# Three projections of a two-block layer with tokens on the partitions, and top-k moved to follow its scores

## The reference, cut

```python
# first block, after two attentions on h = rms(x) @ w_in
mix = concat([rms(o_sb, g1), rms(o_mla, g2)]) @ w_o          # output projection, 1024 x 1024
x = x + rms(mix, g_post_mix)
u = causal_conv3(rms(x, g_pre_ffn) @ w_up)                   # 1024 x 5632
gate, val = split(u)
x = x + rms((gelu(gate) * val) @ w_down, g_post_ffn)         # 2816 x 1024
g = sigmoid(rms(x, g_ple_gate) @ w_ple_gate + b_ple_gate)    # 1024 x 1024
x = x + rms(g * (p @ w_ple), g_post_ple)                     # 256 x 1024
# second block
mod = silu(c) @ mod_w + mod_b                                # 1024 x 6144: six rows of scales and shifts
h = rms(x, norm1_g) * (1 + sc1) + sh1
# z = h @ w_in_2 feeds a 31-tap convolution, a pool mixer, and an attention that keeps, of each
# token's index scores, the 64 best keys
x = x + g1 * (concat(parts) @ w_out_2)
# 32 experts of width 512, two for each token
x = x + g2 * moe(rms(x, norm2_g) * (1 + sc2) + sh2)
return rms(x, final_g)
```

## Time and profile before

| | |
|---|---|
| time, median of 3 runs | 1084.17 us (1083.63 to 1092.6) |
| time of the profiled execution | 1083.46 us |
| its span, first to last instruction | 1081.4 us |
| TensorE busy | 847.7 us (78%) |
| VectorE, ScalarE, POOL busy | 322.7, 284.2, 141.1 us |
| mean granted TensorE clock | 0.913 of full speed |
| DMA | 297.44 MB, mean 275 GB/s |

### The profile page before, as it was taken

How to read it: one execution, slowest core, us unless ns; L and a number is a source line. 1 busy time by engine, 2 the same in 40 slices (tenths; PEclk the granted TensorE clock), 3 DMA queues, 4 the chain that set the end, 5 groups by cost and what they waited for, 6 DMA issues and landing times.

```text
span 1081.4 us, 12688 instructions
## 1 busy us (share of the span) xinstructions
PE 847.7 (78%) x5392; PEld 577.1 (53%) x5392; DVE 322.7 (30%) x674; ACT 284.2 (26%) x541; POOL 141.1 (13%) x152
## 2 busy tenths in 40 slices
PE   7998688799998998959977979866657665766564
PEld 6855366699998995838765945312113131212111
DVE  2215422567666424054754131000001010000001
ACT  2325321366566442223534121000000000000011
...
GB/s 364 376 145 100 167 212 223 166 161 205 182 160 123 210 22 428 178 78 79 137 174 1 396 188 360 429 428 427 428 427 428 428 427 427 429 427 429 427 427 179
DMA packets 22671, 297.44 MB, mean 275 GB/s; under 512 B 2640, under 2 KB 2896, under 8 KB 4560
## 3 DMA queue, kind: packets, MB, share of 16 engines
...
HBM read 295.50 MB, written 1.05 MB: 274 GB/s over the span
## 4 chain that ended last, share of the span: by engine, by line
PE 57%; DMA 28%; DVE 8%; ACT 4%; issue 1%; POOL 1%; SPq 0%; DVEq 0%; POOLq 0%
PE ps L186 56%; DMA ring<-in_exps 28%; DVE yT L214 1%; ACT ar L200 1%; DVE ar L206 1%; DVE hT L214 1%; ACT yT L200 1%; DVE rb L275 1%; ACT ar L197 1%; DVE ar L1086 0%; ACT sq L200 0%; DMA ring<-in_win 0%; DVE yT L206 0%; DVE misc L1083 0%; DVE misc L615 0%
## 5 line engine op out<-in xcount | busy, mean ns | idle before, releaser
L186 PE MATMUL ps<-ring,sq 128*32 128x512 f32 x976 | 140.8, 712 | 90.3 <-DMA ring<-in_exps 88.6
L186 PE MATMUL ps<-hT,ring 128*128 128x256 f32 (+2 forms) x672 | 152.2, 388 | 12.9 <-DMA ring<-in_win 6.8
L186 PE MATMUL ps<-ring,ar 128*32 128x512 f32 (+1 forms) x696 | 100.9, 691 | 58.8 <-DMA ring<-in_exps 35.2
L186 PEld LDWEIGHTS ps<-hT,ring 128*128 128x128 f32 (+2 forms) x672 | 128.6, 192 | 34.2 <-issue 7.6
L186 PEld LDWEIGHTS ps<-ring,sq 128*32 128x32 f32 x976 | 29.8, 120 | 197.1 <-DMA ring<-in_exps 138.0
L186 PE MATMUL ps<-fr 128*128 128x256 f32 x792 | 103.2, 287 | 7.0 <-DVE fr L206 7.0
L186 PE MATMUL ps<-fr,fr_h 128*128 128x256 f32 x792 | 101.8, 284 | 4.0 <-POOL fr_h L217 2.1
L186 PEld LDWEIGHTS ps<-fr 128*128 128x128 f32 x792 | 99.7, 196 | 7.4 <-issue 6.4
L186 PEld LDWEIGHTS ps<-fr,fr_h 128*128 128x128 f32 x792 | 98.5, 192 | 4.5 <-POOL fr_h L217 2.3
L200 ACT ACTIVATE ar<-ps 128x768 f32<-128x768 f32 (+1 forms) x21 | 15.1, 717 | 281.1 <-PE ps L186 276.0
L206 DVE TENSOR_TENSOR ar<-ar,ps 128x512 f32<-128x512 f32 (+1 forms) x10 | 6.4, 641 | 267.8 <-PE ps L186 267.8
...
## 6 DMA issues: line engine op xcount, KB each, us to landing
...
```

The source lines that it names most:

```text
L186: return pe(lambda e: e.matmul(o, l, r, start=start, stop=stop, skip_group_check=True), *waits, inc=inc)
```

## The change

The output projection, down and gate now load the activations (128 features x 128 tokens) and stream 512 columns of the weights, so the result has tokens on the partitions, in four banks (token half j, column half n): `wo_part`, `down` and the gate's loops. The norm's sum then runs along a row: `token_square` squares with an accumulator, `token_diagonal` adds two numbers per token, takes root and reciprocal of one column, and writes the identity scaled by the factors. `to_features` multiplies the copied result (`mt`, in `yT`) by that diagonal, which turns it back and scales it, and `add_turned` adds it to `xT` with the gain, on VectorE. The next norm's sums take the loaded squares against one column of ones (`x_sums`), root and reciprocal are of two columns (`row_root`), and `over_rows` spreads the factors over the partitions. The gate's factor and bias are applied on its result, the bias from a new input `brow`.

Slot 5 moves to the last place of `mla_fill`, 6, 7 and 8 to 11 between the new steps; `mod_sum(7)` goes behind up's first slot and `mod_sum(11)` behind the first projection of the second block. Four weight parts of up are made ahead instead of two. The six slots of down are asked for at once, and the loads of `pT` and `brow` behind them wait for the end of up. `modulated` adds its shift on ScalarE, and the first projection of the second block goes over features first. The top-k's rounds are placed on VectorE behind the index scores: four there, three behind the latent norms' sums, one behind the latents. At the end a table load for the root is issued before the last squares; an activation that loaded it in the last expert group goes. The functions `Norm` and `residual` are removed.

```diff
         def mla_fill(i):
             if i == 1:
                 sb_group()
-            elif i < 6:
+            else:
                 mod_slot(i - (i > 1))
...
+        def row_root(b, dim, c, t):
+            m = misc[:, c:c + 4]
+            read[b] = t = a_fn(m[:, 0:2], ps[:, b, 0:2], ACT.Sqrt, t, t_eps, bias=eps, scale=1.0 / dim)
+            return m[:, 2:4], dve(lambda e: e.reciprocal(m[:, 2:4], m[:, 0:2]), t)
+        def over_rows(b, r, *waits):
+            for j in range(2):
+                t = mm(bank(b, 128 * j, 128 * j + 128), r[:, j:j + 1].broadcast_to([128, 128]), ident, True, True, *waits, inc=j)
+            return t
+        part, fac, mt, dg = misc[:, 56:60], misc[:, 72:78], yT, rb[:, 0, :]
+        def token_square(j, n, src, *waits):
+            i = 2 * j + n
+            return a_fn(sq[:, 512 * i:512 * i + 512], src, ACT.Square, *waits, accum_out=part[:, i:i + 1])
+        def token_diagonal(j, *waits, beside=None):
+            t = v_tt(fac[:, j:j + 1], part[:, 2 * j:2 * j + 1], part[:, 2 * j + 1:2 * j + 2], ALU.add, *waits)
+            if beside:
+                beside()
+            t = a_fn(fac[:, 2 + j:3 + j], fac[:, j:j + 1], ACT.Sqrt, t, t_eps, bias=eps, scale=1.0 / 1024)
+            t = dve(lambda e: e.reciprocal(fac[:, 4 + j:5 + j], fac[:, 2 + j:3 + j]), t)
+            return v_ts(dg[:, 128 * j:128 * j + 128], ident, fac[:, 4 + j:5 + j], None, ALU.mult, None, t, d_con)
+        def leave(j, n, b, t, t_sq, t_mt, t_dg, *waits):
+            i = 2 * j + n
+            t_sq[j, n] = token_square(j, n, bank(b), t)
+            def copy():
+                read[b] = t_mt[j, n] = v_copy(mt[:, 512 * i:512 * i + 512], bank(b), t_sq[j, n], *waits)
+            if n:
+                t_dg[j] = token_diagonal(j, t_sq[j, 0], t_sq[j, 1], beside=copy)
+            else:
+                copy()
+        def to_features(j, TB, *waits):
+            out = []
+            for k in range(8):
+                b = TB[k // 2]
+                o = (k % 2) * S + 128 * j
+                t = mm(bank(b, o, o + 128), mt[:, 1024 * j + 128 * k:1024 * j + 128 * k + 128], dg[:, 128 * j:128 * j + 128], True, True,
+                       read[b] if j == 0 else None, *waits, inc=k % 2)
+                out += [t] if k % 2 else []
+            return out
+        def add_turned(TB, gain, tt):
+            out = []
+            for k in range(8):
+                b, x = TB[k // 2], tile(xT, k)
+                t = v_stt(x, bank(b, (k % 2) * S, (k % 2) * S + S), gain(k), x, ALU.mult, ALU.add, tt[0][k // 2], tt[1][k // 2], d_cols)
+                read[b] = t
+                out.append(t)
+            return out
+        def x_square(i, tx_):
+            return a_fn(sq[:, i * 512:(i + 1) * 512], xT[:, i * 512:(i + 1) * 512], ACT.Square, tx_[2 * i + 1])
+        def x_sums(i, b, tok):
+            for k in (2 * i, 2 * i + 1):
+                for j in range(2):
+                    o = k * S + 128 * j
+                    t = mm(ps[:, b, j:j + 1], sq[:, o:o + 128], ones[:, 0:1], k == 0 and j == 0, k == 7, tok,
+                           read[b] if k == 0 and j == 0 else None, inc=int(k % 2 == 1 and j == 1))
+            return t
...
+        def wo_part(j, n, ks):
+            for k in ks:
+                o = k * S + 128 * j
+                t = mm(bank(2 * j + n), hT[:, o:o + 128], w_o[n].ap(k * 512, 512), k == 0, k == 7, w_o[n].ready, tg[k],
+                       read[2 * j + n], inc=int(k == ks[-1]))
             return t
+        for n in range(2):
+            for j in range(2):
+                wo_part(j, n, range(4))
...
+        t_sq, t_mt, t_dg = {}, {}, {}
+        for n in range(2):
+            for j in range(2):
+                t = wo_part(j, n, range(4, 8))
+                leave(j, n, 2 * j + n, t, t_sq, t_mt, t_dg)
+            w_o[n].free(t)
+        t_oT.append(t)
+        ahead += [weight_parts(w_up.ap(512 * k, 512), p_tt, w_up.ready) for k in range(2, 4)]
+        TB = (6, 7, 0, 1)
+        tt = [to_features(j, TB, t_dg[j], t_mt[j, 0], t_mt[j, 1]) for j in range(2)]
+        t_x = add_turned(TB, lambda k: col("g_post_mix", k), tt)
+        sqd = [x_square(i, t_x) for i in range(4)]
+        mod_slot(6)
+        for i in range(4):
+            t = x_sums(i, 2, sqd[i])
+        r, t_r = row_root(2, 1024, 116, t)
+        t = over_rows(3, r, t_r, read[3])
+        tx = []
         for k in range(8):
+            th = v_stt(tile(yT, k), tile(xT, k), col("g_pre_ffn", k), bank(3, 0, S), ALU.mult, ALU.mult, t, tt)
+            tx.append(split(tile(yT, k), tile(fr, k, XH), tile(fr, k, XL), v_tt, th))
+        read[3] = th
+        mod_slot(7)
...
+                                  weight_parts(w.ap(512 * k, 512), p_tt if k % 4 == 3 or (j == 0 and k % 2) else v_tt, w.ready))
...
+            if j == 0:
+                mod_sum(7)
...
+        t_up = t
+        DB = {(0, 0): 2, (0, 1): 3, (1, 0): 6, (1, 1): 7}
+        w_d = [stream("wdown", i, (4 if i < 5 else 2) * 1024) for i in range(6)]
+        pT, eT, brow = 0, 512, 2560
+        d_p = sp.dma(lambda e: e.dma_start(ar[:, pT:pT + 512], A["pT"]), sem("s_p"), 16, t_up)
+        d_b = sp.dma(lambda e: e.dma_start(ar[:, brow:brow + 1024], A["brow"]), sem("s_b"), 16, t_up)
...
+        def down(f, j, n, wh, wl, t_w):
+            fh, fl = (fr[:, o + S * f + 128 * j:o + S * f + 128 * j + 128] for o in (FH, FL))
+            o = bank(DB[j, n])
+            mm(o, fh, wh, f == 0, False, t_w, t_f[f], read[DB[j, n]])
+            mm(o, fh, wl, False, False)
+            return mm(o, fl, wh, False, f == 21, inc=1)
+        t_sq, t_mt, t_dg = {}, {}, {}
+        for f in range(20):
+            for n in range(2):
+                i, wh, wl, t_w = down_parts(f, n)
+                for j in range(2):
+                    t = down(f, j, n, wh, wl, t_w)
+                wp_free[i] = t
+                next(behind, None)
+            if f % 4 == 3:
+                w_d[f // 4].free(t)
+            if f == 8:
+                a_fn(misc[:, 2:3], eps, ACT.Sqrt, t_eps)
+        for n in range(2):
+            wps = [down_parts(f, n) for f in (20, 21)]
+            for j in range(2):
+                for f, (i, wh, wl, t_w) in zip((20, 21), wps):
+                    wp_free[i] = t = down(f, j, n, wh, wl, t_w)
+                leave(j, n, DB[j, n], t, t_sq, t_mt, t_dg, conv_prev)
+        w_d[5].free(t)
+        t_down = t
+        spread_cond(t)
+        w_p = stream("wple", 0, 2048)
+        t_e = {}
+        def embed(j, n):
+            b = 4 + j
+            t = chain(bank(b), [(ar[:, pT + k * S + 128 * j:pT + k * S + 128 * j + 128], w_p.ap(k * 1024 + 512 * n, 512))
+                                for k in range(2)], w_p.ready, d_p, read[b])
+            o = eT + 1024 * j + 512 * n
+            read[b] = t_e[j, n] = a_copy(ar[:, o:o + 512], bank(b), t)
+            return t
+        embed(0, 0)
+        TB = (0, 1, 2, 3)
+        tt = [to_features(j, TB, t_dg[j], t_mt[j, 0], t_mt[j, 1]) for j in range(2)]
+        t_x = add_turned(TB, lambda k: col("g_post_ffn", k), tt)
+        th = [a_fn(tile(hT, k), tile(xT, k), ACT.Copy, t_x[k], t_down, scale=col("g_ple_gate", k)) for k in range(8)]
+        embed(1, 0)
+        embed(0, 1)
+        w_p.free(embed(1, 1))
+        sqd = [x_square(i, t_x) for i in range(4)]
+        mod_slot(8)
+        ZB = {(0, 0): 6, (1, 0): 7, (0, 1): 0, (1, 1): 1}
+        t_gz, t_sq, t_dg = {}, {}, {}
+        w = stream("wgate", 0)
+        for k in range(8):
+            for j in range(2):
+                o = k * S + 128 * j
+                t_gz[j, 0] = mm(bank(ZB[j, 0]), hT[:, o:o + 128], w.ap(k * 512, 512), k == 0, k == 7, w.ready, th[k],
+                               read[ZB[j, 0]], inc=int(k == 7))
+            if k == 3:
+                for i in range(4):
+                    t = x_sums(i, 3, sqd[i])
+                r3, t_r3 = row_root(3, 1024, 120, t)
+        w.free(t_gz[1, 0])
+        w = stream("wgate", 1)
+        for j in range(2):
+            for k in range(8):
+                o = k * S + 128 * j
+                t = mm(bank(ZB[j, 1]), hT[:, o:o + 128], w.ap(k * 512, 512), k == 0, k == 7, w.ready, read[ZB[j, 1]], inc=int(k == 7))
+            t_gz[j, 1] = t
+        w.free(t)
+        for n in range(2):
+            for j in range(2):
+                b, i = ZB[j, n], 2 * j + n
+                y, g = mt[:, 512 * i:512 * i + 512], ar[:, eT + 512 * i:eT + 512 * i + 512]
+                read[b] = t = v_stt(y, bank(b), r3[:, j:j + 1], ar[:, brow + 512 * n:brow + 512 * n + 512], ALU.mult, ALU.add,
+                                    t_gz[j, n], t_r3, d_b, tt)
+                t = a_fn(y, y, ACT.Sigmoid, t)
+                if n and j:
+                    a_fn(misc[:, 2:3], eps, ACT.Sqrt, t_eps)
+                t_mt[j, n] = v_tt(y, y, g, ALU.mult, t, t_e[j, n])
+                t_sq[j, n] = token_square(j, n, y, t_mt[j, n])
+                if n:
+                    t_dg[j] = token_diagonal(j, t_sq[j, 0], t_sq[j, 1])
```

(38 more changed lines are left out.)

203 lines of the change are left out of this document (24 added, 179 removed).

## The result

The changed kernel took 1053.68 us (median of 4 runs, 1047.83 to 1054.28) against 1084.19 us (4 runs, 1083.63 to 1092.6): the ratio is 0.969, with a 95% interval from 0.963 to 0.975. It is faster, as forecast, and by less: 30.5 us instead of 44, so that it lies 0.7 us above the upper end of the range. The profiled execution took 1053.41 us with a span of 1051.4, against 1083.46 and 1081.4.

The account below looks back on a forecast made before the run. TensorE work with holes bounds the path to the DMA-bound expert weights, so an earlier start brings the end forward equally. 10.7 - 1.9 + 5.3 + 17.9 + 1.5 + 9.1 + 1.3 = 43.9 us gained: 1040 us, range 1031 to 1053.

Parts of the forecast that it names:

- 1. Output projection to up: From the first block's output projection to up's first matmul: up starts at 193.9 instead of 204.56 us, 10.7 us gained.
- POOL's collision with the diagonal: Before up: POOL's third weight part could hold the ports shared with VectorE, diagonal up to 1.3 us later, total 1041.
- 2. Up: Up's matmuls: VectorE's late share of the fifth weight part leaves a 3.2 us hole; 132.1 us in all, 1.9 lost.
- 3. Down: Down's matmuls: 264 wide fp32r ones at 0.217 us plus holes, 63.6 instead of 68.9 us, 5.3 gained.
- 4. Down to the second block: Down's end to the second block's projection: 62.8 instead of 80.7 us, 17.9 gained; that projection's 144 records 1.5 faster.
- 5. Top-k: Second block's index top-k: rounds fit VectorE's idle gaps, first mask at 557.5 instead of 566.66 us, 9.1 gained.
- 6. End: Kernel's end: the 1.28 us table load goes in front of the last squares, 1.3 us gained.
- The leaking joints: Rival: six chains of small operations (three diagonals, three roots) each end 2 us after their cover; 1052 us, chance 0.10.
- The wide form: Rival in down: the 512-column fp32r matmul pays the floor twice, 0.240 us, losing 6.1; 1046 us, chance 0.07.
- Top-k did not stay on the path: Rival in the second block: moved rounds delay the factors behind them, giving back 9.1 us; 1049 us, chance 0.07.
- wide matmuls did not overlap: Rival in down: a 512-column matmul costs 0.120 us like a 256-column one, shrinking down by 25.6; 1014 us, chance 0.02.
- the slower rival: Rival in down: wide fp32r runs at f32's rate, 0.87 us a matmul, down takes 229 us; 1212 us, chance 0.03.

Follow-up runs that it names:

- the second profile: The changed kernel run and profiled once more with nothing altered: 1050.93 us (1045.8 to 1053.88), ratio 0.964 to the kernel before; profiled span 1046.5 us.
- 128 columns: Changed kernel with its sums of squares streaming 128 columns of ones instead of one, at three places: 1048.06 us, ratio 0.961 to the kernel before.
- the long fillings: Changed kernel with 128-column sums plus extra unread matmuls where TensorE idles, twice as long as meant: 1050.45 us, ratio 0.964 to the kernel before.
- the best version: Changed kernel with 128-column sums, interleaved splits ahead of up, and unread matmuls lengthened to close the softmax gaps: 1035.61 us, ratio 0.9495 to the kernel before.

## Why the prediction was right, and where it was short

The sign and the mechanism held. The table sums up to 30.0 us instead of 43.9, and 1.6 of the 30.0 are luck: the first softmax, which nothing changed, was that much faster in this execution (142.90 instead of 144.48; 144.59 in the second profile).

**1. Output projection to up (forecast 10.7, got 7.3).** The working up to the sums is confirmed nearly to the tenth: half 1 is turned 2.13 us after half 0 (2.3 forecast), the joint at the root is 0.55. POOL's collision with the diagonal did not come: the diagonal was made by 178.7 us, when POOL had just begun, and the turn waited for 0.18. By the rule of the Trainium skill ("SBUF — State Buffer", section "SBUF: two separate sides") it could have been 1.3 us late, by the estimate of the prediction; no run here shows that it was. The term that failed is "Sums of squares: 16 matmuls, 32 records x 0.125 = 4.0" with slot 7 behind it at 2.9: they took 5.82 and 4.9. The records' own price was right (3.63 at full clock); what they do to the clock was not in the sum. With 128 columns the way is 48.40, 1.0 better than forecast.

**2. Up (forecast 1.9 lost, got 0.8 lost).** From 195.72 to 326.67 us it takes 130.95, against 132.1. The hole of 3.2 us at the fifth weight part was 1.26 only because up started late; with up on time it was 3.17, as worked out. The step that was too kind is that a hole costs its own length: behind it 24 records ran at the lower clock in one profile (4.64), and at the full one in another after as long a hole, that of the long fillings:

```profile
208.16 3.13 PE L186 MATMUL ps<-fr 128*128 128x256 f32 x24 [3.16 <-DVE fr L210]
```

**3. Down (forecast 5.3, got 2.7).** The wide fp32r matmul takes 0.2267 us: where nothing is waited for, groups of twelve start 2.72 us apart.

```profile
346.91 2.88 PE L186 MATMUL ps<-fr 128*128 128x512 f32 x12
349.63 2.88 PE L186 MATMUL ps<-fr_h,fr 128*128 128x512 f32 x12
```

That is between the bounds of 0.217 and 0.240, and 264 x 0.0097 is 2.6 us, the whole difference: 66.16 instead of 63.6. I had scaled from the f32 rows. The two fp32r prices, 0.120 for 256 columns and 0.2267 for 512, come, if the price is a straight line through these two, to 0.107 for each 256 columns and 0.013 for each matmul; my scaling had no such second part. What is left beside the matmuls' price is 6.3 us, as forecast in sum but not one by one: POOL's hole was 2.41 instead of 3.2, that of the last parts 2.10 instead of 2.4. And this execution was lucky: its last twelve records took 3.02 us behind the hole of 2.10, while in the eight other profiles of this form of down they took 4.55 to 4.62 behind the same hole.

**4. Down to the second block (forecast 17.9, got 14.9; the 144 records forecast 1.5 faster, got 0.8 slower).** No joint leaked: TensorE idles 0.55 us in all between slot 10 and slot 11. The loss is the clock again, 1.7 in the gate, some 3 up to slot 11, some 3 in the projection (none there in the second profile, 69.49 us). At full clock the stretch is 60.90, so the working, 62.8, was on the safe side.

**5. Top-k (forecast 9.1, got 9.0).** Right to the tenth, in the whole change, undone, and alone. Behind the mask this execution lost 1.4 us to slow score records (66.79 against 65.41), the second profile nothing (65.43).

**6. End (forecast 1.3 gained, got 2.0 lost).** The table load is off the tail: the root follows the last read at once, where 1.28 us stood between them in the earlier trace rows.

```profile
1044.00 0.19 ACT L200 ACTIVATION_READ_ACCUMULATOR hT<-ps 128x1 f32 x1
1044.09 0.28 ACT L200 ACTIVATE misc<-misc 128x1 f32<-128x1 f32 x1
```

But in this execution the last sixteen expert records took 3.64 us instead of 1.92 and the last eight 5.41 instead of 3.70. In the second profile both are at full clock, and the end is 1.44 shorter than before, the forecast's 1.3.

**The rivals.** The leaking joints (1052) came nearest in time and were wrong in mechanism: the six chains ended under their covers. The wide form lies between the forecast's price and that rival's. Top-k did not stay on the path, wide matmuls did not overlap, and the slower rival did not come. What was missing is a rival of its own: that the new short records and the remaining idle time lower TensorE's clock. Rows for the idle half were there: the first 24 records of up at twice the price after 6.30 us of idleness, and 0.84 in a window. I booked them as costs of the old kernel that the change removes, 1.5 us of them as a gain, and did not ask where the new one would make such stretches. That one-column records bring the fall no row of the kernel before shows.

What stays open: what it is in the one-column sums that goes before the fall; only one, 128 and 256 columns were tried. In the best version the clock also fell from 1.00 to 0.50 at 573.8 us, in the router's records of 36 columns and of one, with TensorE busy without a gap, and sixteen records behind them took 3.65 us; in both profiles of the changed kernel the clock stayed at 1.00 there and these sixteen took 1.94. Nor is it known why one hole of 3.2 us was followed by slow records and another was not. The records of down behind its last hole (4.61 us for twelve) are slow even in the best version.
